# Two places of a two-block transformer kernel: what runs before and after a phase border in the opening, and where the router's table products stand in TensorE's queue

## The reference, cut to what matters

```python
# first layer: modulation, then a normalised input of the attention projections
mod = (silu(c) @ ada_w[layer] + ada_b[layer])[:, None, :]
sh_a, sc_a, gt_a, sh_m, sc_m, gt_m = jnp.split(mod, 6, axis=-1)
h = modulate(rms_norm(x, attn_norm[layer]), sh_a, sc_a)
...
q, k, v = jnp.split(h @ w_in, 3, axis=-1)
...
# mixture of experts: each row goes to its two best experts of its group
weights = top_p / jnp.sum(top_p, axis=-1, keepdims=True) * p_gsel
order = jnp.argsort(flat_e)
...
xs = jnp.zeros((rows, d), h.dtype).at[dest].set(hf[stok])
hid = jax.nn.silu(xb @ w_gate[e]) * (xb @ w_up[e])
return hid @ w_down[e]
```

## Time and profile before

| what | value |
|---|---|
| median of 3 runs | 2323.35 us (2322.1 to 2327.71) |
| the profiled execution, its own time | 2324.44 us |
| its span | 2322.7 us |
| TensorE busy | 2224.3 us (96%) |
| VectorE, ScalarE, GpSimd busy | 1222.7, 519.2, 41.4 us |
| transfers | 452.07 MB, mean 195 GB/s |
| mean granted clock of TensorE | 0.983 |

### The profile page before, as it was taken

The page is one execution under the profiler, slowest core; times in us unless marked ns, Lnnn a source line. Parts: engine busy times, 40 slices in busy tenths (PEclk is TensorE's granted clock), DMA queues, the critical chain, the costliest instruction groups (busy, mean ns, idle before and its releaser), DMA issues. The chain is left out here.

```text
span 2322.7 us, 26623 instructions
## 1 busy us (share of the span) xinstructions
PE 2224.3 (96%) x9804; PEld 1495.5 (64%) x9804; DVE 1222.7 (53%) x2805; ACT 519.2 (22%) x1188; POOL 41.4 (2%) x49
## 2 busy tenths in 40 slices
PE   8999999999999999999999999999999899999985
PEld 4444688888887555558888888854578544444332
DVE  5455666667766365676655767668565311111104
ACT  4333223230003244442333100112232100000001
POOL 0000000000000000000000000000000010000100
PEclk9999999999999999999999999999998999999999
DMA  9455223534433211113534435422032799999996
GB/s 361 170 199 199 73 73 150 212 146 179 184 145 118 73 55 55 51 50 149 211 149 179 184 147 200 161 73 73 1 145 90 298 427 426 427 426 425 426 426 250
DMA packets 46419, 452.07 MB, mean 195 GB/s; under 512 B 7560, under 2 KB 8840, under 8 KB 21456
## 3 DMA queue, kind: packets, MB, share of 16 engines
q1 hardware_dynamic: 39440, 436.04, 47.1%
q0 software_dynamic: 6240, 12.17, 1.4%
q10 hardware_dynamic: 608, 2.14, 0.2%
HBM read 443.36 MB, written 17.87 MB: 199 GB/s over the span
## 5 line engine op out<-in xcount | busy, mean ns | idle before, releaser
L1404 PE MATMUL ps<-big,ring 128*128 128x256 f32 x768 | 186.0, 379 | 0.6 <-PE ps L1319 0.6
L3299 PE MATMUL ps<-big 128*64 128x512 f32 (+1 forms) x416 | 171.7, 607 | 7.8 <-ACT big L3355 5.0
L1319 PE MATMUL ps<-hT,ring 128*128 128x256 f32 x768 | 178.3, 381 | 0.0
L1319 PEld LDWEIGHTS ps<-hT,ring 128*128 128x128 f32 x768 | 144.8, 190 | 23.1 <-ACT hT L452 4.0
L1404 PEld LDWEIGHTS ps<-big,ring 128*128 128x128 f32 x768 | 145.6, 190 | 21.0 <-issue 1.4
L584 PE MATMUL ps<-hT,ring 128*128 128x512 f32 x336 | 151.7, 600 | 0.0
L3299 PE MATMUL ps<-ring,big 128*64 128x512 f32 (+1 forms) x336 | 135.7, 600 | 11.4 <-ACT big L3355 6.6
L2333 PE MATMUL ps<-hT,ring 128*128 128x512 f32 x320 | 140.7, 594 | 2.7 <-DVE big L2715 1.7
L1216 DVE SCALAR_TENSOR_TENSOR ring<-ring,tmp 128x1024 f32<-128x1024 f32 x112 | 136.3, 1217 | 0.0
L1404 PE MATMUL ps<-oT 128*128 128x256 f32 x512 | 120.8, 379 | 2.1 <-DVE oT L1583 2.1
L1319 PE MATMUL ps<-oT 128*128 128x256 f32 x512 | 115.8, 379 | 0.0
(11 more groups left out here) (555 smaller groups left out, 3887.6 us busy)
## 6 DMA issues: line engine op xcount, KB each, us to landing
ring<-in_stream SPq DMA_DIRECT2D x98, 2048.0 KB, 8.8
big<-in_up SPq DMA_DIRECT2D x18, 2048.0 KB, 22.6
ring<-in_down SPq DMA_DIRECT2D x17, 2048.0 KB, 22.2
ring<-in_gate SPq DMA_DIRECT2D x15, 2048.0 KB, 22.8
big<-in_gate SPq DMA_DIRECT2D x10, 2048.0 KB, 20.4
big<-in_down SPq DMA_DIRECT2D x8, 2048.0 KB, 22.1
ring<-in_up SPq DMA_DIRECT2D x6, 2048.0 KB, 19.0
oT<-in_up SPq DMA_DIRECT2D x5, 2048.0 KB, 28.2
```

Of the source, the lines that this page charges most:

```text
L1319: ins = pe.matmul(place(i, name), a[:, k, :], b[:, k, :], start=(k == 0), stop=(k == 3))
L1404: ins = pe.matmul(m.ps[:, bank[name], q * H:(q + 1) * H], a[:, q * P:(q + 1) * P], b, start=(first and q == 0), stop=(final and q == 1))
L3299: ins = pe.matmul(out[a:z, :], left[:, k * P + a:k * P + z], bufs[j][:, k * width + c * 512:k * width + (c + 1) * 512], start=(k == 0), st ...
```

## The change

Three edits:

1. `keep_busy` behind the sums of squares issues 2 products, not 6.
2. VectorE makes only rows j = 0 and 1 of chunk 0 before the border. Rows j = 2 and 3 are made past it, behind `unit_rows(0)`, and with them goes the increment of `free[0]`. ScalarE's waits follow: k tile 1 now waits for `first_done` 2, k tile k for 2k (the same rows as before for k of 2 and more).
3. In the router the eight table products stand ahead of k tile 5 of the gate product, not of k tile 2.

```diff
@@ phase_start, VectorE
                 dve.reciprocal(m.st[:, 0:NT], m.st[:, 0:NT]).then_inc(inverse, 1)
-                for j in range(2, 4):
-                    first_modulation(m, dve, 0, j, crow).then_inc(mod_done, 1)
-                dve.wait_ge(mod_done, 4)
-                dve.sem_inc(m.free[0], 1)
+                dve.wait_ge(mod_done, 2)
@@ phase_start, TensorE
-                keep_busy(m, pe, 0, 6)
+                keep_busy(m, pe, 0, 2)
@@ phase_diff, ScalarE
                 for k in range(KT):
-                    if k >= 2:
-                        act.wait_ge(first_done, 2 * k - 2)
+                    if k:
+                        act.wait_ge(first_done, 2 * k)
@@ phase_diff, VectorE
                     n = ada_chunk(c)
-                    dve.wait_ge(m.full[n % RING], 16 * (n // RING + 1))
-                    for j in range(4):
-                        first_modulation(m, dve, c, j, crow).then_inc(first_done, 1)
-                    dve.wait_ge(first_done, 4 * c)
+                    if c:
+                        dve.wait_ge(m.full[n % RING], 16 * (n // RING + 1))
+                    for j in range(4 if c else 2):
+                        first_modulation(m, dve, c, j if c else 2 + j, crow).then_inc(first_done, 1)
+                    dve.wait_ge(first_done, 4 * c + 2)
                     dve.sem_inc(m.free[n % RING], 1)
...
-                for c, tiles in ((1, range(0, 3)), (2, range(3, 6)), (3, range(6, KT))):
+                for c, tiles in ((0, range(0, 1)), (1, range(1, 3)), (2, range(3, 6)), (3, range(6, KT))):
@@ phase_route, TensorE
-                        if j == 0 and k == 2:
+                        if j == 0 and k == 5:
```

## The result

| | before | after |
|---|---|---|
| time, median of 20 runs each | 2322.91 us (2317.72 to 2328.09) | 2328.49 us (2321.63 to 2336.71) |
| ratio | | 1.0025 [1.0016, 1.0033] |
| profiled execution's own time | 2324.44 us | 2324.04 us |
| its span, mean granted clock | 2322.7 us, 0.983 | 2322.3 us, 0.980 |

The change made the kernel 5.6 us slower, where 3.6 us faster was forecast. The profiled execution of after doesn't show it: at 2324.04 us it stands 4.4 us under the median of its kernel, so it can tell where each local term went, but not where the median's 5.6 us came from. The runs further down had to tell that.

The account below looks back on a forecast made before the run. TensorE was taken as the bound from opening to router, transfers behind it. Terms +0.7 and -4.3 us sum to -3.6, from a median of 2323.35 to 2319.8 us; range 2317.0 to 2323.4.

Parts of the forecast that it names:

- The border is 1.07 us earlier.: Opening: with eight fewer warming passes, the spread behind them ends at 21.75 us instead of 22.82.
- +0.7 us: Opening: the moved rows delay tile 6, so the first projection ends at 48.2 us against 47.47.
- So what the opening gains or loses is carried to the router whole.: Between opening and router: TensorE is the bound, so the opening's +0.7 us reaches the router unchanged.
- The rival of a falling clock: Clock falls in the new gaps: 2321.4 us with one stretch in the opening, 2323.0 with another at the gather; chance 0.15.
- The wait of 2.57 us is filled, and the clock has no gap to fall in: Router: gap ahead of the table products shrinks to some 0.15 us; they take 2.05 us, ending 1.64 us earlier.
- -4.3 us: Router: the phase ends at 1831.6 us instead of 1835.90, including a new wait for the gather.
- The gather, 5.8 us and a wait of 1.0.: Router: first gather lands 5.8 us after issue, at 1827.0 us, and TensorE waits 1.0 us ahead of the transposes.
- this rival: Router: a gather of 10.2 us idles TensorE 5.4 us and the clock falls, giving 2328.4 us; chance 0.06.
- lands in the lull; nothing waits for it: Router: the load behind `gate_used` is issued some 5.7 us earlier, at no cost.
- The queues of the opening at nothing: Opening: later issue of ring buffer 0's load and small transfers costs nothing; up to 2 us if cover were gone.
- the tail: Behind the router: experts' loads all shift equally; the rival that the tail absorbs the gain gave 2323.4 to 2324.0, chance 0.10.
- The sum of -3.6: Whole kernel: +0.7 us in the opening and -4.3 us in the router, giving 2319.8 us on the median.

Follow-up runs that it names:

- the copy of before: The kernel before, unchanged, timed again against itself as a control: ratio 0.9995 [0.9985, 1.0004].
- the opening run again: Edits 1 and 2 alone against the kernel before, run a second time: 2327.61 us, ratio 1.0016 [1.0006, 1.0026].
- the ten traces above: Ten traces of kernels with the router of before; the clock fell behind the 2.57 us gap in three and held in seven.
- the parts: Parts of the change against the kernel before: edit 3 alone 2324.78 us, edits 1 and 2 alone 2327.93, edit 1 alone 2323.99.
- five cut runs: Kernel before cut short, without and with edits 1 and 2, five runs each: 1110.21 and 1110.03 us behind second attention, 1731.80 and 1736.36 behind mixing block.
- Plain delays: Kernel before plus 3, 7 or 13 unread 128-column products in head 1 (0.8, 1.8, 3.3 us): 2324.44, 2323.66, 2326.47 us against 2323.63.

## Why the prediction was wrong, step by step

- *"The border is 1.07 us earlier."* Right. From the start of the warming products to the spread's end it is 3.98 us before and 21.46 - 18.56 = 2.90 after, 1.08 less.
- *The opening, "+0.7 us".* Nearly right as a local term. From the start of the warming products to the end of the projection it is 28.63 us before and 29.66 after, 1.0 more; in the copy of before and the opening run again 28.5 and 29.7. Most of the rest is the last 12 passes, 5.42 us where 12 x 0.43 = 5.16 was taken. The waits were forecast at 1 us each; the first is 0.51 to 1.26 us in four traces, the second 0.5. In after the time won at the border lies at 1.2 GHz (the clock is 0.50 to 25.5 us and 0.59 from there to 28.7), so TensorE gets only half of its passes done in it, and has less to wait away later.
- *"So what the opening gains or loses is carried to the router whole."* **This step failed.** I had drawn it from the waits: no transfer among them, TensorE the bound. But TensorE's rate isn't fixed between the two places. After is 0.75 us behind before at the first head, 0.24 ahead at the mixing block, 3.4 behind at the gate. On the median the edits went with 4.1 to 4.4 us against their groups, where +0.7 was carried. In the traces the lag changes where the clock is at 1.2 GHz in one execution and not in the other. The rival of a falling clock had looked for it in the new gaps of the opening and at the gather only; in the opening's gaps it didn't fall, at the gather it fell in one trace of three. Why the edits cost this much, and where, stays open.
- *"The wait of 2.57 us is filled, and the clock has no gap to fall in", "-4.3 us".* Right for the profiled pair (-4.6), and **mis-sized as a term of the median**. Some 3.1 us of it were the price of a fall that happened in the profiled execution and not in others; where the clock holds, as in seven traces of ten, the edit is worth 1.5 to 2.1 us. I took the one execution for all of them. Measured alone the edit came out at +1.2 us, with an interval of -1.4 to +4.9 us that excludes -4.3.
- *The gather, 5.8 us and a wait of 1.0.* Right in two traces of three (0.80 and 0.83 us); in the third it took 11.3 us. I gave this rival 0.06. It takes back 8.3 us in an execution in which it happens (-4.6 to +3.7), and the ten traces above make the edit worth 2.4 to 2.9 us on average with the gather in time (0.3 x 4.6 + 0.7 x 1.5 to 2.1, an estimate): one late gather in three or four executions undoes that. The load that "lands in the lull; nothing waits for it" was put at nothing. It went out 5.6 us earlier against the gate, as forecast, but that is into the gather's flight.
- *The queues of the opening at nothing, and the tail.* Right: no wait on ring buffer 0 in the opening, and from the first expert pass to the end of the span it is 485.4 to 486.5 us in the traces of before, of after and of the parts.
- *The range and the signs.* 2328.49 lies above 2323.4. The sum of -3.6 would have been +0.7 - 1.5 = -0.8 without the fall, and no term held the 4 us that go with the opening's edits. The median's 0.25% is inside the 0.3% that I called no change, but its interval reaches past it, to 0.33%, and the direction was wrong.

## What to carry to other kernels

Before a fallen clock is costed as a gain, look for the same gap elsewhere in the program and in more than one execution: if passes behind it are sometimes at full speed, the gain is only that share of it. In a kernel like this one, with a dozen places where the clock can fall, the lag between two executions changes by several microseconds on the way, so a term of one microsecond at the start can't be carried to the end, and a forecast's range should hold that scatter with both signs. When a loss is traced to a place, ask runs and traces both: here five cut runs each pointed behind 1110 us and the traces ahead of it. When a product is brought forward, ask what it lets go: here a 2 MB load that then flies with the gather that TensorE needs next.

## What was new about the hardware

- The same gap ahead of the same passes is followed by the full clock in one execution and by 1.2 GHz in the next: 2.57 us in the router (1.99 us for the 16 table passes in seven traces, 3.69 in three), 1.67 us in the mixing block (7.13 or 8.83 us for 16 passes). Such a stretch costs 1.7 us at its place, and in this case part of it was given back further on.
- The first gather took 5.7 to 6.1 us to land in the four traces in which no further 2 MB load went out before it landed, and 5.3 to 7.7 us, once 11.3, in the ten in which one did.
- Two edits in the opening go with a median 4 us longer, in two groups of runs, though on the span's clock the opening ends no later with them (48.44 us against 48.57, means of five traces). Plain delays came out up to 1.8 us under what they add, and with the edits in place once 3.4 us under.
